# Compressed attention in a decoder kernel: one product for values and block importance, row factors turned on TensorE, later loads issued between stores

## The reference, cut to what matters

```python
s = jnp.einsum('bqghd,bngd->bghqn', qc, kc).astype(jnp.float32) * scale
...
p_cmp = masked_softmax(s - sl * dist, valid) * jnp.any(valid, axis=-1)[:, None]
o_cmp = jnp.einsum('bghqn,bngd->bqghd', p_cmp, vc)
imp = jnp.einsum('bghqn,nm->bgqm', p_cmp, a_sel)
...
_, idx = lax.top_k(imp, k_sel)
...
return gc[..., 0:1] * o_cmp + gc[..., 1:2] * o_sel + gc[..., 2:3] * o_win
```

## Time and profile before

| | |
|---|---|
| time, median of 3 runs | 3106.92 us (3104.01 to 3111.18) |
| the profiled execution's own time | 3105.75 us |
| its span, first to last instruction | 3103.9 us |
| the stage, first instruction to the last of the choice | 916.4 to 1047.0 us |
| busy in these 130.6 us | PE 81.3, DVE 94.6, ACT 65.4, POOL 56.5 us |
| first product of the next stage | 1050.5 us |

### The profile page before, as it was taken

How to read it: one execution, slowest core, us unless ns; L and a number is a source line. 1 busy time by engine, 2 the same in 40 slices (tenths; PEclk the granted TensorE clock), 3 DMA queues, 4 the chain that set the end, 5 groups by cost and what they waited for, 6 DMA issues and landing times. The chain is left out here.

```text
span 3103.9 us, 41336 instructions
## 1 busy us (share of the span) xinstructions
PE 2788.5 (90%) x14110; PEld 1911.2 (62%) x14111; DVE 1689.6 (54%) x3401; ACT 1102.8 (36%) x2274; POOL 1039.1 (33%) x1019
## 2 busy tenths in 40 slices
PE   8989999999976799999999899999899999569990
PEld 4668888888864465665545566666444455456670
DVE  6675557655547666666565578878222222422237
ACT  0012222222235355555545456666211122123232
POOL 1267667767713402112130211100122333033333
PEclk9999999999987699999999999999999999689995
DMA  3333234223363101110010121100664243355848
GB/s 132 130 130 109 102 109 175 97 102 109 103 194 135 36 8 59 38 64 12 29 75 21 38 65 42 42 1 1 222 164 115 89 163 126 135 223 208 352 157 338
DMA packets 147479, 345.35 MB, mean 111 GB/s; under 512 B 13536, under 2 KB 61280, under 8 KB 141152
## 3 DMA queue, kind: packets, MB, share of 16 engines
q1 hardware_dynamic: 132080, 286.87, 26.7%
q0 software_dynamic: 12672, 46.14, 4.1%
q10 hardware_dynamic: 2544, 9.96, 0.9%
HBM read 230.01 MB, written 112.92 MB: 110 GB/s over the span
## 5 line engine op out<-in xcount | busy, mean ns | idle before, releaser
L566 ACT ACTIVATE p_kept<-p_a 128x256 f32<-128x256 f32 x336 | 128.5, 383 | 462.4 <-PE p_a L512 462.4
L1536 DVE CUSTOM_DVE_ANT_0 b_prob_s<-b_pq,b_sel 128x640 f32<-128x640 f32 (+5 forms) x192 | 168.6, 911 | 132.2 <-PE b_pq L1428 125.5
L1389 POOL TENSOR_TENSOR b_rate<-gates,b_total 128x256 f32<-128x256 f32 x64 | 37.8, 612 | 582.8 <-DVE b_total L1550 582.8
L1464 PE MATMUL b_po<-b_probT,vsw 128*64 128x256 f32 (+1 forms) x1824 | 232.5, 373 | 0.0
L1831 DVE CUSTOM_DVE_ANT_0 d_prob<-d_pq,d_bias 128x1024 f32<-128x1024 f32 (+6 forms) x192 | 168.0, 909 | 69.1 <-PE d_pq L1723 67.1
L1488 ACT ACTIVATE b_prob_s<-b_prob_s,b_neg 128x1152 f32<-128x1152 f32 (+15 forms) x128 | 152.7, 1194 | 128.6 <-DVE b_neg L1544 128.5
L1428 PE MATMUL b_pq<-ks,b_q 64*128 64x512 f32 (+3 forms) x688 | 167.6, 550 | 18.5 <-PEq L60 9.8
L1559 DVE COPY b_probT<-b_pt 128x512 f32<-128x512 f32 (+1 forms) x253 | 152.4, 629 | 48.1 <-PE b_pt L1451 47.9
L1723 PE MATMUL d_pq<-d_keys,d_q 64*128 64x512 f32 (+3 forms) x576 | 165.6, 560 | 5.2 <-DVE d_seg_max L1831 4.2
L1451 PE MATMUL b_pt<-ident,b_prob_s 128*128 128x128 f32 x1088 | 158.6, 283 | 7.4 <-DVE b_probT L1559 7.1
L1464 PEld LDWEIGHTS b_po<-b_probT,vsw 128*64 128x64 f32 x1824 | 107.6, 136 | 92.8 <-issue 55.2
(11 more groups left out here) (388 smaller groups left out, 6072.6 us busy)
## 6 DMA issues: line engine op xcount, KB each, us to landing
projT<-p_result SPq DMA_DIRECT2D x64, 512.0 KB, 2.8
p_w<-in_wt SPq DMA_DIRECT2D x16, 1024.0 KB, 7.1
p_w_more<-in_wt SPq DMA_DIRECT2D x16, 1024.0 KB, 6.0
gates_T<-projT SPq DMA_DIRECT2D x64, 256.0 KB, 4.0
wgu<-in_w_gu SPq DMA_DIRECT2D x4, 4096.0 KB, 14.1
wgu<-y SPq DMA_DIRECT2D x32, 512.0 KB, 8.5
p_xin<-in_x SPq DMA_DIRECT2D x16, 512.0 KB, 3.9
mergedT<-m_stage SPq DMA_DIRECT2D x32, 256.0 KB, 3.8
```

The source lines that it names most:

```text
L1464: mm = nc.tensor.matmul(po[u % 2][g * HD:(g + 1) * HD, o:o + w], s.vsw[:, kb, v0 + g * HD:v0 + (g + 1) * HD], probT[:, f % 4, g * w:(g + 1 ...
L1536: nc.vector.tensor_tensor_reduce(out=to, in0=pq[g][:, 0:nb * P], in1=away, scale=slopes[PAIRS * g + i], scalar=-3e38, op0=ALU.add, op1=ALU ...
```

## The change

The probabilities are no longer normalised and gated before they are turned. PE turns the bare exponentials, and `vc` becomes a tile of 96 columns per group: 64 of values and 32 of `overlap`, so that one product gives 96 rows, values and importance, for each group in a bank of its own (`po[0]`, `po[1]`). What was done to rows of 32 to 128 keys is now done to the 96 rows of the product, by a factor tile: POOL spreads 1/sum times gate over 64 columns and 1/sum over 32 (`make_weights`), PE turns this (`spread_weights`, 8 transposes more in each step) through the same banks `pt` as the exponentials, ACT and DVE copy a bank each (`keep_factor`), and DVE multiplies `po` by it (`evict`, now on DVE, two multiplications). The row sums come out of the exponentials themselves (`accum_out`). POOL adds up the 32 importance rows of the four steps (`seen`), PE turns the sum back (`turn_sum`, into `po[0]`), and the choice starts at iteration 4c + 5. The masks of the next stage are made before the last two `add_up`. SP issues the next stage's loads one by one between the stores of steps 3 to 10.

```diff
@@ tiles @@
-        gated = [sb(f"gated{k}", [P, GROUPS, 4, P]) for k in range(2)]
-        plain = sb("plain", [P, GROUPS, 4, P])
-        pbar = [sb(f"pbar{k}", [P, GROUPS, 4, P]) for k in range(2)]
+        weights = sb("weights", [P, 2, 4, GROUPS, ROWS])
+        factor = sb("factor", [P, 2, GROUPS, 512])
-        y = sb("y", [P, 2, 512])
+        y = sb("y", [P, 2, GROUPS, 512])
+        seen = sb("seen", [P, 2, GROUPS, 512])
...
@@ SP @@
-            sp.dma_start(s.ks[:], d["qkT"][T_KS]).then_inc(s.kept_in, 16)
-            sp.dma_start(s.kw[:], d["qkT"][T_KW]).then_inc(s.kept_in, 16)
-            for k in range(2):
-                load_queries(sp, d, s, k)
-            for k in range(2):
-                load_distances(sp, d, s, k)
-            sp.dma_start(s.b_wdist[:], d["win_dist"]).then_inc(s.b_const_in, 16)
             for n, (c, i) in enumerate(steps):
                 sp.wait_ge(evicted, n + 1)
-                sp.dma_start(d["ycT"][i][:, c * 512:(c + 1) * 512], y[:, n % 2, :]).then_inc(stored[n % 2], 16)
+                for g in range(GROUPS):
+                    sp.dma_start(d["ycT"][i][g * HD:(g + 1) * HD, c * 512:(c + 1) * 512], y[0:HD, n % 2, g, :]).then_inc(stored[n % 2], 16)
+                if n == 3:
+                    sp.dma_start(s.ks[:], d["qkT"][T_KS]).then_inc(s.kept_in, 16)
+                    sp.dma_start(s.kw[:], d["qkT"][T_KW]).then_inc(s.kept_in, 16)
+                if n in (4, 5):
+                    load_queries(sp, d, s, n - 4)
+                if n in (6, 8):
+                    load_distances(sp, d, s, (n - 6) // 2)
...
@@ POOL @@
+            def make_weights(n):
+                c, i = steps[n]
+                rate = stat[:, n % 4, 3].rearrange("p g t -> p t g")
+                by = s.gates[:, 4 * c:4 * c + 4, :].rearrange("p t (g i b) -> p b i t g", g=GROUPS, b=3)[:, 0, i]
+                pool.wait_ge(rate_ready, n + 1)
...
+                if n >= 2:
+                    pool.wait_ge(spread, n - 1)
+                    pool.wait_ge(summed, n - 1)
+                nc.gpsimd.tensor_tensor(weights[:, n % 2, :, :, 0:HD], by.unsqueeze(3).to_broadcast([P, 4, GROUPS, HD]),
+                                        rate.unsqueeze(3).to_broadcast([P, 4, GROUPS, HD]), ALU.mult).then_inc(weight_ready, 1)
+                nc.gpsimd.tensor_copy(weights[:, n % 2, :, :, HD:ROWS], rate.unsqueeze(3).to_broadcast([P, 4, GROUPS, NBLK])).then_inc(weight_ready, 1)
...
+            make_weights(0)
             for n in range(NS):
+                if n + 1 < NS:
+                    make_weights(n + 1)
+                if n == NS - 2:
...
+                    for j in range(2):
+                        for g in range(GROUPS):
+                            mask_row(s, nc.gpsimd.tensor_tensor, 0, j, g).then_inc(s.b_first_masked, 1)
                 add_up(n)
...
@@ PE @@
+            def spread_weights(n):
+                pe.wait_ge(weight_ready, 2 * n + 2)
+                pe.wait_ge(copied, n + 1)
                 for g in range(GROUPS):
                     for j in range(4):
+                        mm = nc.tensor.transpose(pt[g][0:ROWS, j, :], weights[:, n % 2, j, g, :], s.ident[:])
+                mm.then_inc(spread, 1)
...
                 if n < NS:
-                    pe.wait_ge(gate_done, n + 1)
-                    turn(gated[n % 2], step_use[n])
+                    turn(n)
                 if 1 <= n <= NS:
                     values(n - 1)
+                if n < NS:
+                    spread_weights(n)
                 if n in sel_turn:
...
+                    turn_sum(sel_turn[n])
...
@@ ACT @@
+            exponentials(0, range(GROUPS))
+            exponentials(1, range(GROUPS))
+            for n in range(NS):
+                copy(n)
                 if n + 2 < NS:
-                    exponentials(n + 2)
+                    exponentials(n + 2, [0])
+                keep_factor(n)
+                if n + 2 < NS:
+                    exponentials(n + 2, [1])
...
@@ DVE @@
+            def keep_factor(n):
+                dve.wait_ge(spread, n + 1)
+                nc.vector.tensor_copy(factor[0:ROWS, n % 2, 1, :], pt[1][0:ROWS].rearrange("p a b -> p (a b)")).then_inc(factor_ready, 1)
+
+            def evict(n):
+                dve.wait_ge(valued, n + 1)
+                dve.wait_ge(factor_ready, GROUPS * (n + 1))
...
+                for g in range(GROUPS):
+                    op = nc.vector.tensor_tensor(y[0:ROWS, n % 2, g, :], po[g][0:ROWS, :], factor[0:ROWS, n % 2, g, :], ALU.mult)
+                op.then_inc(evicted, 1)
...
+            rates(0)
             for n in range(LAST):
-                if n < NS:
-                    gate(n)
+                if n + 1 < NS:
+                    rates(n + 1)
                 if n + 2 < NS:
                     maxima(n + 2)
+                if 1 <= n <= NS:
+                    evict(n - 1)
+                if n < NS:
+                    keep_factor(n)
                 if n in sel_choice:
                     choose(*sel_choice[n])
```

More of the change, by code:

```diff
@@ L987, in importance, with values @@
                 for g in range(GROUPS):
                     for j in range(4):
[L989 to L990 removed]
+                        mm = nc.tensor.transpose(pt[g][0:ROWS, j, :], weights[:, n % 2, j, g, :], s.ident[:])
+                mm.then_inc(spread, 1)
+            def values(n):
+                w = width(n)
+                pe.wait_ge(copied, n + 1)
+                if n == 0:
+                    pe.wait_ge(s.select_in, 48)
+                else:
+                    pe.wait_ge(evicted, n)
+                ready = [c for at, c in sel_turn.items() if at <= n]
+                if ready:
+                    pe.wait_ge(weighed, ready[-1] + 1)
+                for g in range(GROUPS):
+                    mm = nc.tensor.matmul(po[g][0:ROWS, :], s.vc[0:w, g, :], probT[0:w, n % 2, g, :], start=True, stop=True)
+                mm.then_inc(valued, 1)
@@ L992, in _, with turn_sum @@
+            def turn_sum(c):
+                pe.wait_ge(summed, PAIRS * (c + 1))
+                pe.wait_ge(evicted, min(PAIRS * (c + 1) + 1, NS))
+                for g in range(GROUPS):
+                    for j in range(4):
+                        mm = nc.tensor.transpose(pi[:, g, j, :], seen[HD:ROWS, c % 2, g, j * P:(j + 1) * P], s.ident[HD:ROWS, HD:ROWS])
+                mm.then_inc(sum_turned, 1)
             scores(0)
@@ L1023, in exponentials @@
                     for j in range(4):
                         x = prob[n % 4][:, g, j, 0:width(n)]
-                        op = nc.scalar.activation(x, x, ACT.Exp, bias=stat[:, n % 4, 1, g, j:j + 1], scale=slopes[PAIRS * g + i])
-                op.then_inc(exp_done, 1)
-            def copy(out, use, free):
-                act.wait_ge(turned, use + 1)
-                if free:
-                    act.wait_ge(valued, free)
+                        op = nc.scalar.activation(x, x, ACT.Exp, bias=stat[:, n % 4, 1, g, j:j + 1], scale=slopes[PAIRS * g + i],
+                                                  accum_out=stat[:, n % 4, 2, g, j:j + 1])
@@ L1032, in copy @@
+                if g == GROUPS - 1:
+                    op.then_inc(exp_done, 1)
+            def copy(n):
+                w = width(n)
+                act.wait_ge(turned, n + 1)
+                if n >= 2:
+                    act.wait_ge(valued, n - 1)
                 for g in range(GROUPS):
-                    op = nc.scalar.activation(out[:, g, :], pt[g][:].rearrange("p a b -> p (a b)"), ACT.Copy)
+                    op = nc.scalar.activation(probT[0:w, n % 2, g, :], pt[g][0:w].rearrange("p a b -> p (a b)"), ACT.Copy)
@@ L1042, in _ @@
             act.wait_ge(s.vsw_in, 16)
             nc.scalar.activation(s.gates[:], s.vsw[:, :, V_GATE:V_DIFF], ACT.Sigmoid).then_inc(gates_ready, 1)
-            exponentials(0)
-            exponentials(1)
-            for n in range(LAST):
-                if n < NS:
-                    copy(probT[:, n % 2], step_use[n], values_at[n - 2] if n >= 2 else 0)
-                if 1 <= n <= NS:
-                    evict(n - 1)
-                if n in sel_turn:
-                    c = sel_turn[n]
-                    copy(sumT, sum_use[c], weights_at[c - 1] if c >= 1 else 0)
+            exponentials(0, range(GROUPS))
```

144 lines of the change are left out of this document (52 added, 92 removed).

## The result

| | before | after |
|---|---|---|
| time, median of 6 runs each | 3105.47 us | 3124.15 us (3120.39 to 3128.02) |
| ratio, with its 95% interval | | 1.0061 [1.0048, 1.0073] |
| the profiled execution's own time | 3105.75 us | 3120.39 us |
| first product of the stage to first product of the next | 916.40 to 1050.53, 134.1 us | 918.55 to 1065.93, 147.4 us |
| differential attention's first product over `d_keys` to the merge's first | 1786.71 to 2202.52, 415.8 us | 1797.77 to 2218.39, 420.6 us |

The change makes the kernel slower by 0.6%, 18.7 us. The forecast was 3104.4 us, in a range of 3093 to 3118. In the profiled executions the stage itself takes 13.3 us more, and a place 1200 us later, just ahead of the merge, 4.8 us more.

What follows compares the result with a forecast made beforehand. DVE was taken to bound the long middle, a late store the hole; closing it gives 12.6 us, 10 go on waiting elsewhere, so the stage ends 2.5 us earlier: 3104.4 us, range 3093 to 3118.

Steps and rivals of the forecast that it cites:

- PE does not limit it: In the changed stage's steps, PE's four groups take 4.4 us in all, within periods of 4.9 to 6.7 us.
- PE at the low clock: Rival for the stage's steps: PE becomes the bound at 7.9 us a step; 16 us more, 3120; chance 0.18.
- groups of eight of 1.97 us: Sign on PE in the changed stage: if its groups take 1.97 us throughout, the clock decides.
- The turn-taking: In the stage's steps DVE and ACT wait for each other; period 4.9, 5.2, 6.0, 6.7 us in chunks 0 to 3.
- The hole: Stretch from 941.7 to 954.3 us where nothing computes; loads issued behind stores remove all 12.6 us.
- POOL's part: POOL's work per step: spreading weights 1.05 us, a copy 0.5, adding 32 partitions by 1024 2.35.
- the cheap rival: POOL's sum of 32 partitions costs 1.2 us and choices are not held; 10 us less, 3094; chance 0.28.
- 3.22: Rival: POOL's sums take their full shown length, 3.22 us each; some 6 us more, 3111; chance 0.10.
- Additions of the choice: DVE's additions in the choice meet a busy POOL and wait; four choices before step 15's bias cost 9 us.
- The gain of DVE alone: If DVE stayed the bound, the stage's middle would gain some 15 us on top of the hole.
- The end: After step 15's bias at 1011.5: masks 8.8 us, two sums 4.8, turn 2.0, last choice 4.1; stage ends at 1044.5.

Runs made afterwards that it cites:

- a_rows: The changed kernel with the product of values alone over all 128 rows in every chunk, turns left narrow; ratio 1.0001 to before, stage 128.7 us.
- b_loads_pool: The kernel before with the next stage's loads between the stores and POOL's add_up waiting for DVE's gate; ratio 0.9942 to before, stage 114.1 us.

## Why the prediction was wrong

- *"PE does not limit it: scores, turn, values and weights are about 1.1 us each at the high clock, 4.4 in all."* This step failed, twice over. "I hold it unlikely for the whole stage" rested on gaps ahead of PE, and in the changed kernel there was no gap at all. The rival, PE at the low clock, is the case that happened, and the sign given for it, groups of eight of 1.97 us, was seen in chunks 0 and 1. That its 3120 us lie so near 3124 is partly luck: it had 7.9 us for every step, where chunks 0 and 1 took 9.25 and the others were not bound by PE. a_rows shows the size: without the low clock the stage is 18.7 us shorter and the time as before (1.0001).
- *The turn-taking* was right: with the clock cured the steps of a_rows are 4.9 us in chunk 0 (7.9 in the one during which the clock rose), 5.0 to 5.2 in chunk 1, 5.7 to 6.1 in chunk 2 and 6.49 in chunk 3 (forecast 4.9, 5.2, 6.0, 6.7), the choices included it is 84.1 us from the bias of step 2 to that of step 15 (forecast 85.3), and the stage is 5.4 us shorter than before, where 2.5 were forecast.
- *"The hole goes, all 12.6 us"*: the hole went, but was worth 17.1 us in the kernel before. Together with a_rows this splits the stage, in this order of the parts (in another the shares differ, since late loads are worth nothing while PE is at the low clock): late loads -17.1, the new attention +11.7 (128.7 against 117.0), narrow rows +18.7, in sum +13.3. The forecast had the first two in effect (-12.6 and +10.1).
- *POOL's part*: the sum of 32 partitions took 2.35 us, as chosen; the cheap rival (1.2) fell, and so did 3.22. Additions of the choice took 0.29 to 2.06 us.
- *The gain of DVE alone*, "some 15 us", is about 12 us by the prediction's own terms (0.7 more a step in chunk 0 to 2.2 less in chunk 3, evenly between). The forecast does not use it.
- *The end* had its masks, sums and waiting as described: 30.0 us from the last bias to the end of the choice, 33.0 forecast.
- *Nothing was expected outside the stage.* 4.8 us came, in the profiled executions, with the second load of `overlap`. No step of the prediction looked at the queue's later users.

## What to carry to other kernels

Cutting a product to the rows that matter takes no time off PE here (at the high clock 1.95 us over 64 rows and 1.88 over 128), and by the clock it made the stage 18.7 us longer. Look at the granted clock of every stretch in which PE is busy without a gap, and try whole tiles first. Count the columns of products that share PE: two groups of 64 ran side by side, two of 96 one after the other. When a change has several parts, time each alone: the late loads alone were worth 0.5%, and the rest of the change hid it.

## What the runs showed of the hardware

- PE was busy in 48.5 of 48.5 us at a granted clock of 0.50 to 0.51 with products over 32 and 64 rows (changed kernel, 941.5 to 990 us), and the same stream with products over 128 rows had 1.00 and 0.94 (a_rows).
- A DVE operation of 128x8 elements with two operands in SBUF took 2.01 us beside POOL's addition (b_loads_pool) and 0.17 alone. The Trainium skill, page "SBUF — State Buffer", section "Who interferes with whom", says that the one that starts second is blocked; the trace agrees: it started 0.37 us behind POOL's addition of 2.35 and ended 0.03 us behind it.
- POOL's addition over 32 partitions by 1024 took 2.35 us, as long as one over 128 partitions by 1024 (b_loads_pool).
- A load of 16 KB issued 1200 us earlier decided in all 20 profiles whether three loads of 1 MB took 3.5 to 5.0 or 8.8 to 10.5 us to issue.
